# A two-block network on one core: memory for each high part of the Hyena spectrum, and the rotated query tile first

## The chip, the cores and the metric
The kernel runs on one core of a Trainium2 chip, in one launch. The metric is device time in microseconds (us); lower is better. The engines are TensorE (PE, matmuls), VectorE (DVE), ScalarE (ACT), GpSimd (POOL) and SyncE (SP, which issues the DMAs). Each runs its own instruction stream in order, and they meet at semaphores.

## What is computed
One sequence of 512 tokens with 1024 features, in fp32, goes through two blocks. The first has a convolution beside a forgetting attention, a cross attention to a memory and an MLP. The second has two layers, and the change is in one part of each: latent attention (layer 1) and the Hyena mixer (layer 2). Cut to these:

```python
# latent attention: 8 heads, 128 plain and 64 rotated dimensions
q = (rms_norm_2(c_q, g_q) @ w_uq).reshape(b, s, MLA_HEADS, QK_NOPE_DIM + QK_ROPE_DIM)
q_nope = q[..., :QK_NOPE_DIM]
q_rope = apply_rope(q[..., QK_NOPE_DIM:], cos[:, :, None], sin[:, :, None])
...
sc = (jnp.einsum('bqhd,bkhd->bhqk', qn, k_nope) + jnp.einsum('bqhr,bkr->bhqk', qr, k_rope))
p = jax.nn.softmax(sc.astype(jnp.float32) * scale, axis=-1).astype(v.dtype)

# Hyena: a long convolution by spectra, of two orders, each followed by a gate
u = dwconv_centred(x @ w_in, w_short)
v, g1, g2 = jnp.split(u, 3, axis=-1)
z = v.astype(jnp.float32)
for o, gate in enumerate((g1, g2)):
    k_f = jnp.fft.rfft(two_sided_kernel(filt[:, o, 0], filt[:, o, 1]), n=n, axis=0)
    z_f = jnp.fft.rfft(z, n=n, axis=1)
    y = jnp.fft.irfft(z_f * k_f, n=n, axis=1)[:, :length]
    z = gate.astype(jnp.float32) * (y + d_bias[o].astype(jnp.float32) * z)
return z.astype(x.dtype) @ w_o
```

## The kernel before
**Three matmuls for one.** Every fp32 operand is split into a high part (rounded to `fp32r`, a copy by ACT) and a low part (the rest, a subtraction by DVE or POOL). `mm3` (L140) multiplies low by high, high by low and high by high into one PSUM bank. Weights come in chunks of up to 1 MB through two buffers `W32` (`CHUNKS` lists them in order, L44 to L62); for chunk n `weights(n)` is in four programs: SP loads it once the parts of chunk n-2 are made, ACT makes the high part, POOL the low part (DVE a half of it where n is in `SHARED`).

**Order of the work.** Five functions, `tensor_program`, `scalar_program`, `vector_program`, `pool_program` and `sync_program`, write the order of each engine by hand. A step that is moved in one of them moves past all that stands between. PSUM banks are taken in turn (`open_bank`), and a bank is opened when its last tenant has been read.

**Latent attention** runs over four pairs of heads. For pair p PE makes the query tiles m = 0, 1 (plain parts of the two heads) and m = 2 (the rotated part of both), copies of which are `QNH` and `QRS`. It then swaps halves of `QRS` by a matmul with `SWAP`, makes the keys (chunk `ukv`), and goes on with the transposes, the logits and the values of earlier and later heads. ACT's `nope(p)` first calls `weights` for the next chunk and then copies the two plain tiles, `query(p)` copies the rotated one. DVE's `turn_q(p)` rotates it, `rotated(p)` makes its low part.

**Hyena.** For each order o in (0, 1): PE transforms (`to_spectrum`), eight groups of row m and half c, each with a real and an imaginary bank. DVE multiplies a group with the filter's spectrum in four instructions (`products`, the filter rows lie in `KB`), POOL adds these in pairs into `YF[k]`, k = 2m and 2m+1, one instruction each. ACT copies the high part `YH[k]` (`y_high`), DVE subtracts the low part `YL[k]` (`y_low`); in order 0 it also makes the low part of the imaginary pieces of the inverse matrix (`inverse_low`). PE transforms back over eight output tiles m and eight steps k (`istep`), three matmuls of 256 columns each. From each tile DVE makes the new z, DVE or POOL (by `gated_here`) multiplies it by the gate, and in order 0 POOL folds it (`z_turn`) and PE transposes it for the next transform; in order 1 ACT and DVE split it into `HYH` and `HYL` for the output product with chunks `hy_o`. The four-slot rings of `YH` and `YL` lie in the memory of the transform's operand `ZH`, `ZL`, and the waits say so:

```python
if k >= 4:
    act.wait_ge(*at("y_used", o, k - 4))
elif k == 0:
    act.wait_ge(*at(*(("zi", 0, 7) if o else ("hy", 23))))
else:
    act.wait_ge(*at("zf", o, 3, 1, 1))
```

The residual input `X` is kept in DRAM during the block (its memory holds filter rows) and comes back with one DMA, `xl`. The SP queue issues in this order: filter rows of both orders (`load_kb`), `xl`, the four chunks `hy_o`, then the up-projection's chunks.

## Time and profile before

| | |
|---|---|
| median of 3 runs (lowest, highest) | 2204.59 us (2202.55, 2209.34) |
| the profiled execution's own time | 2210.78 us |
| its span | 2208.9 us |
| PE, DVE, POOL, ACT busy | 95%, 59%, 42%, 38% |
| chain that ended last | PE 64%, DVE 23%, ACT 9% |
| latent attention with its queries, keys and values | about 870 to 1056 us |
| Hyena, transforms to output product | about 1622 to 1797 us |

A busy share is time in which an engine ran an instruction; PE's matmuls are pipelined, so two that overlap are both shown in full length and the step from start to start is what one costs. In a timeline the bracket gives the idle time before an instruction and the engine whose signal ended it.

### The profile page before, as it was taken

Reading aid. Unit: us, or ns where it says so; the run is one execution under the profiler, and the core shown is the slowest. Engines: PE = TensorE matmul, PEld = TensorE weight load, DVE = VectorE, ACT = ScalarE, POOL = GpSimd, SP = SyncE. Lnnn points to the kernel's source line nnn. Section 1 sums busy time; section 2 is a strip of 40 time slices with the busy share of each in tenths; the row PEclk is TensorE's granted clock in tenths of the full one; section 3 lists DMA queues with packets and bytes.
Section 4 is the critical chain, followed back from the end, with each engine's and each line's share of the span. In section 5 each row is a group of like instructions: output and inputs, shape, how many; then the busy total and the mean of one; then the engine's idle time right before and its main releaser. Section 6 shows DMA issues by size and latency. Waiting matters only on the chain.

```text
span 2208.9 us, 23694 instructions
## 1 busy us (share of the span) xinstructions
PE 2105.8 (95%) x9729; PEld 1723.4 (78%) x9729; DVE 1313.9 (59%) x1649; ACT 833.4 (38%) x1207; POOL 934.8 (42%) x404
## 2 busy tenths in 40 slices
PE   8999999989999998999999999999998899999997
PEld 5677768778888887787878877878887687887786
DVE  7765871743234434654477786445668647777643
ACT  4633465651122224675333333233322234333322
POOL 4252145554444436112434444444666443443443
PEclk9999779989999998999899999989999999999998
DMA  5322112212222221112122222214231212222221
GB/s 192 146 102 76 39 39 96 77 58 96 96 95 96 96 96 48 50 31 74 58 76 96 96 96 96 96 58 181 96 124 58 96 58 77 95 96 96 96 96 39
DMA packets 34272, 191.96 MB, mean 87 GB/s; under 512 B 3871, under 2 KB 4463, under 8 KB 14900
## 3 DMA queue, kind: packets, MB, share of 16 engines
q1 hardware_dynamic: 34164, 190.44, 24.7%
q8 instruction: 77, 1.26, 0.2%
q14 instruction: 31, 0.25, 0.0%
HBM read 176.72 MB, written 13.64 MB: 86 GB/s over the span
## 4 chain that ended last, share of the span: by engine, by line
PE 64%; DVE 23%; ACT 9%; issue 2%; POOL 1%; DMA 1%; SPq 0%; ACTq 0%; DVEq 0%; POOLq 0%
PE ps L136 58%; DVE TMP L165 9%; DVE TMP L171 6%; PE ps L135 4%; ACT WH L152 4%; ACT TMP L153 1%; ACT PAD L152 1%; PE ps L144 1%; DVE TMP L159 1%; DVE X L171 1%; DVE VG L159 1%; DVE X L159 1%; DVE ps L171 1%; DVE YL L159 1%; POOL WL L159 1%
## 5 line engine op out<-in xcount | busy, mean ns | idle before, releaser
L159 POOL TENSOR_TENSOR WL<-W,WH 128x2048 fp32r<-128x2048 f32 (+3 forms) x157 | 661.3, 4214 | 983.6 <-ACT WH L152 983.6
L136 PE MATMUL ps<-HH,WL 128*128 128x512 f32 (+1 forms) x1408 | 556.0, 395 | 27.1 <-DVE HL L159 7.7
L136 PE MATMUL ps<-HL,WH 128*128 128x512 f32 (+1 forms) x1408 | 547.1, 389 | 0.0
L136 PE MATMUL ps<-HH,WH 128*128 128x512 f32 (+1 forms) x1408 | 546.6, 388 | 0.0
L152 ACT ACTIVATE WH<-W 128x2048 fp32r<-128x2048 f32 (+2 forms) x148 | 274.7, 1856 | 334.0 <-PE ps L136 326.5
L136 PEld LDWEIGHTS ps<-HH,WL 128*128 128x128 f32 x1408 | 271.0, 193 | 95.2 <-issue 30.9
L136 PEld LDWEIGHTS ps<-HH,WH 128*128 128x128 f32 x1408 | 270.7, 192 | 53.7
L136 PEld LDWEIGHTS ps<-HL,WH 128*128 128x128 f32 x1408 | 271.2, 193 | 50.5 <-issue 0.2
L159 DVE TENSOR_TENSOR MRL<-MID,MRH 128x512 fp32r<-128x512 f32 x76 | 177.4, 2365 | 162.4 <-ACT MRH L152 162.4
L165 DVE TENSOR_SCALAR TMP<-PAD,PAR 128x512 f32<-128x512 f32 x88 | 208.9, 2374 | 76.2 <-ACT PAD L152 76.2
L136 PE MATMUL ps<-MRH,WL 128*128 128x512 f32 x608 | 238.5, 392 | 4.5 <-DVE TMP L171 2.3
L136 PE MATMUL ps<-MRH,WH 128*128 128x512 f32 x608 | 236.8, 389 | 0.0
L136 PE MATMUL ps<-MRL,WH 128*128 128x512 f32 x608 | 236.7, 389 | 0.0
L136 PEld LDWEIGHTS ps<-MRH,WL 128*128 128x128 f32 x608 | 114.2, 188 | 29.9 <-ACT PAD L152 3.1
L171 DVE SCALAR_TENSOR_TENSOR TMP<-PAD,PAR,TMP 128x512 f32<-128x512 f32 x176 | 132.3, 752 | 6.2
L136 PEld LDWEIGHTS ps<-MRH,WH 128*128 128x128 f32 x608 | 114.2, 188 | 24.0
L136 PEld LDWEIGHTS ps<-MRL,WH 128*128 128x128 f32 x608 | 114.2, 188 | 23.8 <-issue 0.5
L152 ACT ACTIVATE PAD<-ps 128x512 f32<-128x512 f32 x88 | 51.5, 588 | 182.8 <-PE ps L136 182.8
L159 POOL TENSOR_TENSOR TMP<-TMP,TMP 128x512 f32<-128x512 f32 x47 | 62.1, 1322 | 86.7 <-ACT TMP L153 85.0
L153 ACT ACTIVATE TMP<-TMP 128x512 f32<-128x512 f32 (+1 forms) x54 | 32.8, 608 | 163.5 <-DVE TMP L171 147.3
L171 DVE SCALAR_TENSOR_TENSOR X<-X,ps 128x512 f32<-128x512 f32 (+1 forms) x36 | 22.6, 628 | 118.3 <-PE ps L136 118.2
L159 DVE TENSOR_TENSOR TMP<-ps,TMP 128x512 f32<-128x512 f32 x36 | 24.8, 690 | 112.3 <-PE ps L136 105.6
(355 smaller groups left out, 3348.8 us busy)
## 6 DMA issues: line engine op xcount, KB each, us to landing
W<-in_up SPq DMA_DIRECT2D x44, 1024.0 KB, 4.8
W<-in_down SPq DMA_DIRECT2D x22, 1024.0 KB, 4.8
W<-in_w_up SPq DMA_DIRECT2D x16, 1024.0 KB, 4.8
W<-in_w_down SPq DMA_DIRECT2D x16, 1024.0 KB, 4.8
W<-in_hy_in SPq DMA_DIRECT2D x12, 1024.0 KB, 4.8
kd<-STG SPq DMA_DIRECT2D x36, 256.0 KB, 2.0
KB<-kd SPq DMA_DIRECT2D x8, 1024.0 KB, 5.1
W<-in_win_ag SPq DMA_DIRECT2D x4, 1024.0 KB, 4.8
```

The source lines that it names most:

```text
L135: return self.eng.matmul(out, lhs, rhs, start=start, stop=stop, skip_group_check=True)
L136: return self.eng.matmul(out, lhs, rhs, start=start, stop=stop)
L144: return QUIET if self.eng is None else self.eng.transpose(out, src, ident)
L152: return self.eng.activation(out, src, fn, scale=scale)
L153: return self.eng.activation(out, src, fn, scale=scale, bias=bias)
L159: return QUIET if self.eng is None else self.eng.tensor_tensor(out, a, b, op)
L165: return self.eng.tensor_scalar(out, a, s1, None, o1)
L171: return self.eng.scalar_tensor_tensor(out=out, in0=a, scalar=s, in1=b, op0=o1, op1=o2)
```

## The change
- Hyena: `ZH`, `ZL` have one place for both orders, and so has `YF`. `YL` has the memory of `YF` and is written over it. `YH` has eight buffers for each order, in memory of used weight buffers and filter rows; what each waits for follows. ACT makes six high parts before the output chunk's, not four.
- DVE makes `YL` 1 to 3 after product group 6 (index 5), and the products of groups 7 and 8 come after them. PE takes output tiles (0 to 3), (4, 5), (6, 7) over the first four steps instead of (0 to 3), (4 to 7).
- Filter rows of order 1 go to other buffers, with other waits. POOL starts with output chunk 0 after `yh(1,7)`. DVE gates tiles 0, 3, 7 of order 1 instead of 3 and 7.
- SP loads `hy_o` 0 once the first filter row of order 1 is used, `hy_o` 1 after the first four steps, and `X` in two halves after the inverse transform, ahead of `hy_o` 2 and 3.
- Latent attention: PE makes tile 2 first, then 0 and 1; ACT copies the rotated tile ahead of `nope`.

```diff
...
         for name in ("par", "idt", "mk", "zf", "f1", "fw", "dec", "wf", "e0", "e000", "e001", "e010", "e011",
-                     "tri", "mem", "pos", "swap", "xs", "xl",
+                     "tri", "mem", "pos", "swap", "xs", "xl0", "xl1",
                      *[f"x{k}" for k in range(8)], *[f"aug{q}{g}" for q in range(4) for g in range(2)],
...
         KX = [sb(f"KX{o}", (36, A + 112)[o], [128, 1024]) for o in range(2)]
-        AT = [A + 80, A]
-        ZH = [sb(f"ZH{o}", AT[o], [128, 4, 1024], R) for o in range(2)]
-        ZL = [sb(f"ZL{o}", AT[o] + 16, [128, 4, 1024], R) for o in range(2)]
-        YF = [sb(f"YF{o}", AT[1 - o], [128, 8, 1024]) for o in range(2)]
+        ZH = sb("ZH", A + 80, [128, 4, 1024], R)
+        ZL = sb("ZL", A + 96, [128, 4, 1024], R)
+        YF = sb("YF", A, [128, 8, 1024])
+        YL = sb("YL", A, [128, 8, 1024], R)
         KB = [sb(f"KB{i}", 8 * i, [128, 2048]) for i in range(4)]
-        YH = [[sb(f"YH{o}{i}", AT[o] + 8 * i if i else 32, [128, 1024], R) for i in range(4)] for o in range(2)]
-        YL = [[sb(f"YL{o}{i}", AT[o] + 8 * i + 4 if i else 36, [128, 1024], R) for i in range(4)] for o in range(2)]
+        _w = [16 + 8 * (CH[name][0] % 2) for name in ("dft_z", "dft_i")]
+        YH = [[sb(f"YH{o}{k}", at_, [128, 1024], R) for k, at_ in enumerate((32, 36, _w[o], _w[o] + 4, 0, 4, 8, 12))]
+              for o in range(2)]
         HYH = sb("HYH", A + 80, [128, 8, 512], R)
...
-            return m if o else m % 2
+
+            return 2 + (CH["dft_z"][0] + m) % 2 if o and m < 2 else m % 2
...
-            return m % 4 == 3 if o else m % 2 == 0
+            return m in (0, 3, 7) if o else m % 2 == 0
...
                 wh, wl = chunk(n)
-                for m in range(3):
+                for m in (2, 0, 1):
                     ps = open_bank("uq", p, m)
...
                                      k == 0, k == 2)
-                    ins.then_inc(*up(acc, ("uq", p, m), *[("w_used", n)] * (m == 2)))
-                    if p == 0 and m == 1:
+                    ins.then_inc(*up(acc, ("uq", p, m), *[("w_used", n)] * (m == 1)))
+                    if p == 0 and m == 0:
                         spread("nv", slot=20)
...
                     ins = pe.mm3(ps[:], wh[:, col:col + 128], wl[:, col:col + 128],
-                                 ZH[o][:, odd + kt, half(c)], ZL[o][:, odd + kt, half(c)], kt == 0, kt == 1)
+                                 ZH[:, odd + kt, half(c)], ZL[:, odd + kt, half(c)], kt == 0, kt == 1)
                 ins.then_inc(*up(acc, ("zf", o, m, part, c), *[("w_used", n)] * (o and m == 3 and part * c)))
...
                     pe.wait_ge(*at("yh", o, k))
-                    return pe.mm3(pss[m][:, 256 * h:256 * h + 256], YH[o][k % 4][:, blk(m)], YL[o][k % 4][:, blk(m)],
+                    return pe.mm3(pss[m][:, 256 * h:256 * h + 256], YH[o][k][:, blk(m)], YL[:, k, blk(m)],
                                   wh[:, col:col + 256], wl[:, col:col + 256], k == 0, k == 7, shared=True)
...
-                for q in range(0, 8, 4):
-                    for m in range(q, q + 4):
+                for tiles in ((0, 1, 2, 3), (4, 5), (6, 7)):
+                    for m in tiles:
                         pss[m] = open_bank("zi", o, m)
                     for k in range(4):
-                        for m in range(q, q + 4):
+                        for m in tiles:
                             ins = istep(m, k)
-                        if q:
-                            ins.then_inc(*up(acc, ("y_used", o, k)))
+                ins.then_inc(*up(acc, ("y_used", o, 3)))
                 for k in range(4, 7):
...
                 if p < 3:
+                    query(p + 1)
                     nope(p + 1)
-                    query(p + 1)
                     mla_k(p + 1)
...
                 if o == 1:
-                    act.wait_ge(*at("yh", 0, 7))
+                    act.wait_ge(*at("zf", 0, 3, 1, 1))
                 p3 = bank("tz", o, j)[:].rearrange("p (a c) -> p a c", a=4)
-                high(ZH[o][:, :, blk(j)], p3, ("zh", o, j))
+                high(ZH[:, :, blk(j)], p3, ("zh", o, j))
...
                 act.wait_ge(*at("yf", o, k, 1))
-                if k >= 4:
-                    act.wait_ge(*at("y_used", o, k - 4))
-                elif k == 0:
-                    act.wait_ge(*at(*(("zi", 0, 7) if o else ("hy", 23))))
-                else:
-                    act.wait_ge(*at("zf", o, 3, 1, 1))
-                high(YH[o][k % 4][:], YF[o][:, k, :], ("yh", o, k))
+                if o == 1:
+                    act.wait_ge(*at("zi", 0, 7))
+                if k in (2, 3):
+                    act.wait_ge(*(at("kbu", 1, 1) if o else at("w_low", CH["dft_z"][0])))
+                if k > 3:
+                    act.wait_ge(*at("kbu", o, k // 2))
+                high(YH[o][k][:], YF[:, k, :], ("yh", o, k))
...
                 act.wait_ge(*at("z2", 1, k))
-                act.wait_ge(*at("yh", 1, 7))
+                act.wait_ge(*at("zf", 1, 3, 1, 1))
                 act.copy(HYH[:, k, 0:256], VG[0][:, k, 0:256]).then_inc(*out(("hz", k, "hi1")))
...
             for o in range(2):
-                for k in range(4):
+                for k in range(6):
                     y_high(o, k)
...
                     weights(CH["hy_o"][0])
-                for k in range(4, 8):
-                    y_high(o, k)
+                y_high(o, 6)
+                y_high(o, 7)
                 for m in range(8):
...
                 p3 = bank("tz", o, j)[:].rearrange("p (a c) -> p a c", a=4)
-                low(ZL[o][:, :, blk(j)], p3, ZH[o][:, :, blk(j)], ("zh", o, j), ("free", "tz", o, j))
+                low(ZL[:, :, blk(j)], p3, ZH[:, :, blk(j)], ("zh", o, j), ("free", "tz", o, j))
...
             def y_low(o, k):
-                low(YL[o][k % 4][:], YF[o][:, k, :], YH[o][k % 4][:], ("yh", o, k))
+
+                low(YL[:, k, :], YF[:, k, :], YH[o][k][:], ("yh", o, k))
...
                         z_low(1, 7)
-                    if i == 3:
-                        y_low(o, 0)
-                    if i == 5 and o == 0:
-                        inverse_low(1)
-                    if i == 6:
-                        y_low(o, 1)
-                for k in range(2, 8):
+                    for k in {3: (0,), 5: (1, 2, 3)}.get(i, ()):
+                        y_low(o, k)
+                        if k % 2 and o == 0:
+                            inverse_low(k)
+                for k in range(4, 8):
                     if k % 2 and o == 0:
...
             hy_low(7)
-            dve.wait_ge(*at("xl"))
+            dve.wait_ge(*at("xl0"))
             for n in range(6):
...
                     weights(CH["hy_o"][1])
+                if n == 4:
+                    dve.wait_ge(*at("xl1"))
                 deep(2, "ho", n)
...
                         pool.wait_ge(*at("hy", 23))
-                    pool.tt(YF[o][:, 2 * m, half(c)], q[0], q[1], ALU.subtract).then_inc(
+                    pool.tt(YF[:, 2 * m, half(c)], q[0], q[1], ALU.subtract).then_inc(
                         *out(("yf", o, 2 * m, c), ("tf", "q", o, m, c, 0), ("tf", "q", o, m, c, 1)))
                     pool.wait_ge(*at("yi", o, m, c))
-                    pool.tt(YF[o][:, 2 * m + 1, half(c)], q[2], q[3], ALU.add).then_inc(
+                    pool.tt(YF[:, 2 * m + 1, half(c)], q[2], q[3], ALU.add).then_inc(
                         *out(("yf", o, 2 * m + 1, c), ("tf", "q", o, m, c, 2), ("tf", "q", o, m, c, 3)))
                 if o:
+                    pool.wait_ge(*at("yh", 1, 7))
                     weights(CH["hy_o"][0])
...
                 if o and m >= 2:
-                    n = CH["dft_z"][0] if (CH["dft_z"][0] - m) % 2 == 0 else CH["dft_i"][0]
+                    sp.wait_ge(*at("zi", 0, 7))
+                elif o and m:
+                    n = CH["dft_i"][0]
                     sp.wait_ge(*at("w_high", n))
                     sp.wait_ge(*at("w_low", n))
-                    if n in SHARED:
-                        sp.wait_ge(*at("w_low2", n))
+                    sp.wait_ge(*at("w_low2", n))
                 elif o:
-                    sp.wait_ge(*at("kbu", 0, m + 2))
+                    sp.wait_ge(*at("y_used", 0, 3))
                 elif m >= 2:
...
             sp.wait_ge(*at("kbu", 1, 0))
-            sp.wait_ge(*at("kbu", 1, 1))
-            load("xl", X[:], XD)
-            for m in (2, 3):
-                sp.wait_ge(*at("kbu", 1, m))
-            weights(*range(CH["hy_o"][0], len(CHUNKS)))
+            weights(CH["hy_o"][0])
+            sp.wait_ge(*at("y_used", 1, 3))
+            weights(CH["hy_o"][1])
+            sp.wait_ge(*at("zi", 1, 7))
+            load("xl0", X[:, 0:4, :], XD[:, 0:4, :])
+            load("xl1", X[:, 4:8, :], XD[:, 4:8, :])
+            weights(*range(CH["hy_o"][2], len(CHUNKS)))
             for k in range(8):
```

## Rows read from the trace of the kernel before

**Rows 1.** The page, PE's granted clock in 40 slices of the span, tenths of full speed
```profile
PEclk9999779989999998999899999989999999999998
```

**Rows 2.** Hyena windows: busy us of PE, PEld, DVE, ACT, POOL; PEclk, DMA
```profile
1645.00:1665.00 20.00, 16.71 (x114) 16.07 (x113) 14.20 (x17) 6.11 (x6) 6.76 (x4) 0.83 0.44 167
...
1705.00:1728.00 23.00, 16.34 (x121) 14.89 (x120) 17.51 (x14) 9.00 (x8) 14.42 (x9) 1.00 0.28 96
```

**Rows 3.** Waits from 1600 to 1800 us: who waited for whom, total us, times, longest
```profile
PE ps L135 <- DVE YL L159: 9.9, 9, 2.0
```

**Rows 4.** PE timeline, latent attention: start, us, instruction, idle before and its releaser
```profile
929.12 1.10 PE L136 MATMUL ps<-QRS,SWAP 128*128 128x512 f32 x2 [0.78 <-ACT QRS L152]
...
999.65 0.50 PE L136 MATMUL ps<-KRL,QR 128*128 128x512 f32 x1 [0.65 <-DVE QR L159]
```

**Rows 5.** ACT timeline, Hyena block
```profile
1643.91 2.95 ACT L152 ACTIVATE YH<-YF 128x1024 fp32r<-128x1024 f32 x3 [11.56 <-PE ps L136]
...
1754.62 1.91 ACT L152 ACTIVATE WH<-W 128x2048 fp32r<-128x2048 f32 x1 [2.65 <-PE ps L136]
```

**Rows 6.** PE timeline, inverse transform of order 0
```profile
1647.26 0.40 PE L135 MATMUL ps<-WH,YL 128*128 128x256 f32 x1 [2.02 <-DVE YL L159]
...
1647.46 0.41 PE L135 MATMUL ps<-WL,YH 128*128 128x256 f32 x1
...
1663.01 0.28 PE L135 MATMUL ps<-WL,YH 128*128 128x256 f32 x1
...
1663.13 0.28 PE L135 MATMUL ps<-WH,YH 128*128 128x256 f32 x1
...
1663.87 0.36 PE L135 MATMUL ps<-WH,YL 128*128 128x256 f32 x1 [0.46 <-DVE YL L159]
```

**Rows 7.** DVE timeline, Hyena block
```profile
1640.52 2.49 DVE L159 TENSOR_TENSOR TMP<-ps,KB 128x512 f32<-128x512 f32 x4 [0.20 <-POOL YF L159]
...
1658.14 1.23 DVE L159 TENSOR_TENSOR YL<-YF,YH 128x1024 fp32r<-128x1024 f32 x1 [4.84 <-ACT YH L152]
...
1659.29 0.42 DVE L159 TENSOR_TENSOR WL<-W,WH 128x256 fp32r<-128x256 f32 x1
...
1701.47 2.49 DVE L159 TENSOR_TENSOR TMP<-ps,KB 128x512 f32<-128x512 f32 x4 [0.20 <-POOL YF L159]
...
1719.72 8.18 DVE L159 TENSOR_TENSOR YL<-YF,YH 128x1024 fp32r<-128x1024 f32 x4 [4.61 <-ACT YH L152]
...
1728.63 0.75 DVE L171 SCALAR_TENSOR_TENSOR VG<-VG,SM,ps 128x512 f32<-128x512 f32 x1 [0.72 <-PE ps L135]
...
1749.32 2.10 DVE L159 TENSOR_TENSOR HYL<-VG,HYH 128x256 fp32r<-128x256 f32 x6
```

**Rows 8.** POOL timeline, Hyena block
```profile
1632.70 2.56 POOL L159 TENSOR_TENSOR YF<-TMP,TMP 128x512 f32<-128x512 f32 x2 [0.25 <-DVE TMP L159]
...
1641.89 10.00 POOL L159 TENSOR_TENSOR YF<-TMP,TMP 128x512 f32<-128x512 f32 x6 [0.20 <-DVE TMP L159]
...
1718.82 8.00 POOL L159 TENSOR_TENSOR WL<-W,WH 128x512 fp32r<-128x512 f32 x4 [4.79 <-ACT WH L152]
```

**Rows 9.** The chain that ended last, in order of time: start, us, what
```profile
1681.67 4.34 PE ps L136 x12
...
1689.76 16.60 PE ps L136 x72
```

**Rows 10.** DMA issues: line, engine, count, KB each, us to landing
```profile
X<-xd SPq DMA_DIRECT2D x1, 2048.0 KB, 7.8
```

**Rows 11.** DVE timeline, latent attention, head pair 0
```profile
894.94 1.41 DVE L171 SCALAR_TENSOR_TENSOR TMP<-CQF,PAR,ps 128x512 f32<-128x512 f32 x2 [1.27 <-PE ps L135]
...
899.37 0.69 DVE L159 TENSOR_TENSOR TMP<-ps,CS 128x512 f32<-128x512 f32 x1
```

**Rows 12.** POOL timeline, latent attention
```profile
958.11 2.39 POOL L159 TENSOR_TENSOR WL<-W,WH 128x1024 fp32r<-128x1024 f32 x1 [25.33 <-ACT WH L152]
...
994.45 4.60 POOL L159 TENSOR_TENSOR WL<-W,WH 128x2048 fp32r<-128x2048 f32 x1 [2.15 <-ACT WH L152]
```

## The prediction

> **What bounds the kernel now.** I read the page first: TensorE (PE) is busy for 95% of the span, and its clock is granted nearly in full except in some slices [rows 1]. So time is to be had only where PE stands still or runs at the lower clock. I took windows through the two stretches that the diff touches. In the Hyena block PE is busy for 16.7 of 20 us, and 16.3 of 23 us, while VectorE (DVE) or GpSimd (POOL) is not [rows 2]. The list of waits of 1600 to 1800 us names DVE's low parts of the spectrum, `YL`, as the cause [rows 3]. The PE timeline then gives places. In latent attention the gaps are small and end on the copy of the rotated query, or on `QR` [rows 4].
>
> **Hyena, order 0.** Before, PE finishes the forward transform at about 1643.7 and starts the inverse transform, but high parts 1 to 3 lie in memory that the transform reads, so ScalarE (ACT) copies them only then [rows 5], and DVE takes `YL1` after product group 7, `YL2` and `YL3` after group 8. High parts 4 to 7 wait until PE has used buffers 0 to 3. PE stands 2.02 us for `YL1`, again for `YL2`, then runs for 31 matmuls at a step of 0.20 to 0.21 us instead of 0.12, the lower of the clock's two levels (1.2 GHz for 2.4), and starts the last step of tile 0 at 1663.87 [rows 6].
> Changed: all eight high parts have memory of their own, so ACT follows POOL's sums at once, and DVE does `YL1` to `YL3` after group 6. Prices: a group of four products 2.49 us, `YL` 1.15 us to the start of the next instruction (1659.29 less 1658.14), the low part of a piece of the inverse matrix 0.42 busy, 0.33 to the next start [rows 7], one POOL sum 1.28 (half of 2.56), one matmul of 256 columns 0.12, so 117 of them (8 tiles x 4 steps x 3, three more steps for two tiles, the last for one: 96+18+3) are 14.0 us [rows 6, 8].
> What shares something: POOL's six sums of groups 6 to 8 took 10.00 us instead of 6 x 1.28 = 7.7 while DVE did its `YL` [rows 8]. Both have their two inputs in SBUF. I let such instructions exclude each other and alternate: a `YL` beside a waiting sum costs about 1.27 more.
> DVE ends group 6 at 1643.0 [rows 7]. `YL1` waits 0.15 for POOL and ends at 1644.4; a sum goes between, to 1645.6; inverse low 1, `YL2`, `YL3`, inverse low 3 end at 1648.6 (0.33+1.15+1.15+0.33). Groups 7 and 8 are put back from here and end at 1653.5 (2 x 2.45). `YL4` waits for one sum and ends at 1654.9, a sum to 1656.1, then two inverse lows and `YL5` to `YL7`: 2 x 0.33 + 3 x 1.15 = 4.1, to 1660.3. PE: steps 0 to 3 of tiles 0 to 3 are done at 1650.2, tiles 4 and 5 need the banks of group 7 (1651.1), tiles 6 and 7 follow, to 1657.0; the last step of tile 0 starts at 1660.4. That is 3.4 us before 1663.87; DVE ends last. Below it: 0, if PE runs at the low level again and DVE alternates with POOL at every `YL`; above: 5.9, if PE alone set it (1643.7 + 14.0 + 0.3 = 1658.0). The chain that follows (DVE, POOL's turns, PE's transposes) starts with tile 0 and moves whole. I take 3.4.
> The Trainium skill ("SBUF — State Buffer", on the shared port pair) says that a VectorE instruction with two SBUF inputs and a GpSimd one that reads SBUF take the pair exclusively, for the whole instruction; the trace agrees (10.00 against 7.7 us). If the two only shared a bandwidth pool, without turns, order 0 would come at about 5.9 instead of 3.4 us; it speaks against putting three `YL` in front of products.
>
> **Order 1.** The forward transform ends at 1706.4 (1689.76 + 16.60) [rows 9], in old times. After group 6 (1701.47 + 2.49, less the 0.1 that two instructions overlap: 1703.9 [rows 7]) DVE does `YL1` at 1705.3, a POOL sum, `YL2` 1707.8, `YL3` 1708.9, groups 7 and 8 to 1713.8, `YL4` 1715.2, a sum, `YL5` to `YL7` to 1719.9. There are no inverse lows here. PE needs 14.0 us from 1706.6: 1720.7, so it is just PE that ends last. Before, ACT waited for the output chunk's DMA (the load was behind group 8) and four `YL` took 8.18 us (4 x 1.15 without that) beside POOL's four low parts of that chunk, 8.00 us [rows 7, 8]; the chunk is now loaded after the first row of spectra and POOL waits for `yh(1,7)`. First tile seen by DVE: 1728.63 before [rows 7], 1720.9 now: 7.7 us.
> Paid back in the tail: DVE now gates tile 0, one more of its instructions (0.76), and POOL's low parts of the chunk (4.60 us for such a chunk alone [rows 12], now from 1719.9) lie beside that gate, both with two inputs in SBUF: about 0.5 more. DVE's own chain from 1728.63 to the last three `HYL` at 1749.32 [rows 7] remains the bound of the output product, PE waits for it. Net 7.7 - 1.3 = 6.4. Bounds: 4 (one more alternation in each of the two tiles, and the gate fully late) to 8.
>
> **Waits added, edits at nothing.** POOL's wait for `yh(1,7)` has its low part of output chunk 0 and five gates behind it; PE needs that low part when the inverse is done (1729.7 in old times), it is there at about 1725. SyncE's wait for `y_used(1,3)` and for `zi(1,7)` has `hy_o` 1, both halves of `X`, and `hy_o` 2 and 3 behind it: the 2 MB of `X` landed in 7.8 us [rows 10], with the 1 MB of chunk 2 at that rate 11.7 after the inverse transform, which ended near 1737.3 (tile 0 at 1728.3, then 75 matmuls of 0.12). ACT's copy of chunk 2 came 17.3 us after that, at 1754.62 [rows 5], and the first residual just before: hidden, with 5 us to spare. An overrun would be paid in full. Filter rows (1,0) and (1,1) are now loaded after `y_used(0,3)`, about 1657, 2 MB like `X`, so some 8 us; the products of order 1 start beside PE's run at 1681.67 [rows 9]. Rows (1,2) and (1,3) come after `zi(0,7)`, near 1677, and are used 15 us later. An in-place `YL` is not in the trace; the nearest row is `YL` into other memory, 1.23 us [rows 7]. I take the same and leave 0.1 us either way for each, 1.6 at most over sixteen, little of it on the path. Tile order (4,5), (6,7) has the same matmuls.
>
> **Latent attention.** Pair 0: the rotated tile ends two tiles earlier, so PE's swap no longer waits for its copy, and the key latents' high parts no longer stand behind `QRS` on ACT. DVE's rotation, which starts at 899.37 behind `CVL`, can start at about 897.65 (894.94 + 1.41 [rows 11], and two `CVL` at 0.65 behind ACT's copies, which overlap the 1.41): 1.7 us, and the first logits hang on DVE from there. Pairs 1 to 3: PE is idle for 0.78 us before the swap at 929.12 [rows 4], 0.94 counted from the point at which the next pipelined matmul could have started (928.18); this goes. Next late: the low part of the `ukv` chunk, since ACT's copy of it now stands behind `QRS` (0.5 us). It ended at 958.11+2.39 = 960.5, then 961.0, while PE would want it at 960.5 [rows 12]: pair 2 keeps 0.5. In pair 3 DVE's `QR` is held by POOL's 4.60 us low part of the output chunk from 994.45, which doesn't move, and PE already waits 0.65 for it [rows 4, 12]: the gain is lost there, 0. Sum 1.7+0.9+0.5+0 = 3.1; from 1 (pair 0 half) to 4.6 (1.8 + 3 x 0.94).
>
> **Sum.** 3.4 + 6.4 + 3.1 = 12.9 us. The profiled execution took 2210.78, so 2197.9 on its terms; it is 6.2 above the median of the runs shown, 2204.59, and on that the forecast is 2191.7. About 0.3%, 6.6 us, is what a measurement can tell from no change.
>
> **Rivals.**
> - *The low clock comes back.* A pause of 2.02 us went before the 0.20 us steps in order 0, yet in order 1 PE stood 6.7 of 23 us and was granted full clock (0.83 and 1.00 [rows 2]). PE's pauses get shorter, which speaks against it. Price: 31 matmuls x 0.09 = 2.9 us in order 1, half of that in order 0 where DVE ends last: 12.9 - 4.4 = 8.5, so 2196.1. The 12 matmuls that took 4.34 us instead of 2.7 [rows 9] could as well lose that: 1.6 less, 2190.
> - *DVE and POOL don't take turns as I let them*: order 0 gives 5.9, so 2189.2.
> - *The gain of one part is taken back.* `YL1` to `YL3` move the products, so PE waits for banks before tiles 4 and 6 instead of for `YL`. That holds if POOL's sums delay `YL1` by more than a sum each; then order 0 and most of order 1 give 4 in place of 9.8, with 3.1: 2197.5. That the change does nothing but the attention part: 2201.5. For it: DVE is full in both cases, 17.5 of 23 us.
> - *Slower.* PE's clock stays low over the whole block. It did so elsewhere with PE busy all the time: two slices of 55 us are granted 0.7 to 0.8 [rows 1]. From the inverse transform of order 0 to the last output tile are 154 us; at 0.78 against about 0.95 now that is 154 x 0.17 = 26 us lost, 2218. It beats the gain once more than 13 us, half of that, are lost (a granted clock of 0.87 or less over the block). Against: the 512-column streams around were at full clock.
>
> **Chances.** Forecast 0.62 (alone 2187 to 2196), low clock 0.14, no turns 0.10, taken back 0.10 (half of it within 0.3%), slower 0.04. Faster by over 0.3%: 0.62 + 0.14 + 0.10 + 0.05 less 0.03 for the tails, 0.88; within 0.3% 0.08; slower 0.04. The range: from 18.5 us (4.6+5.9+8), 2186, and a little of a better clock, 2185, to 5.0 (1+0+4), 2199.6.
>
> **What would show it.** Right: `YH` of order 0 starts from about 1632 on one by one and none waits for PE; no pause of PE over 1.2 us in an inverse transform; first tile of order 0 out some 3 us earlier relative to the forward transform's end (20.2 us before), of order 1 14 to 15 instead of 22 us; four `YL` of order 1 in about 6 instead of 8.2 us; no pause before the swap in pairs 1 to 3. Wrong: PE waiting over 2 us for `zf` banks at tiles 4 or 6, a granted clock under 0.9 in these 20 us, residuals waiting for `X`, or output chunk 2 landing after chunk 0 is used.

## The result, and the profile after

| | before | after |
|---|---|---|
| median, us (lowest, highest; 14 runs each) | 2206.63 (2201.17, 2214.91) | 2194.05 (2186.92, 2198.88) |
| the profiled execution's own time / its span | 2210.78 / 2208.9 | 2188.62 / 2186.4 |

The ratio after to before is 0.9937, 95% interval 0.9924 to 0.9950: 13.9 us less by the ratio, 12.6 between the two medians. Forecast were 12.9 us and 2191.7 us, with 2185 to 2199.6 as the range; faster by over 0.3% had 0.88. The direction was right, and the time and the size of the gain are near. Experiments 1 and 2 had one execution each at a far lower granted clock (2626.45 us at 0.738, 7690.57 us at 0.416), and their ratios leave these two out.

The two profiled executions differ by 22.5 us, which is more than the change is worth. The chains of both show where the rest comes from: a stage that the change doesn't touch, long before latent attention, starts its run of matmuls 8 us earlier (506.79 us before, 498.77 after). Up to it the same code was granted another clock; four equal blocks of matmuls took 66.5 us before (214.30 to 280.79) and 60.1 after (213.38 to 273.48), 6.4 of the 8 us. First the kernel before, then after, by windows (columns as in [rows 2]):

```profile
165.00:220.00 55.00, 55.00 (x226) 42.73 (x224) 33.60 (x57) 19.06 (x33) 16.99 (x4) 0.91 0.22 77
220.00:275.00 55.00, 55.00 (x217) 43.09 (x217) 44.30 (x82) 26.75 (x60) 9.15 (x2) 0.78 0.11 39
```
```profile
165.00:220.00 55.00, 55.00 (x241) 43.55 (x240) 35.76 (x62) 19.73 (x35) 17.59 (x4) 0.97 0.22 77
220.00:275.00 55.00, 55.00 (x245) 42.71 (x243) 49.16 (x86) 27.87 (x64) 9.12 (x2) 0.88 0.14 46
```

PE is busy for 55.00 of 55 us in all four lines, but gets through more matmuls at the higher clock (226 and 217 before, 241 and 245 after). So the two spans must not be subtracted. I compare stretches between the same two instructions instead, which start and end inside the changed stages:

| stretch, us | before | after | forecast |
|---|---|---|---|
| latent attention: first query matmul to the first of its output product | 136.32 | 132.98 | -3.1 |
| order 0: first inverse matmul to DVE's first `VG` | 20.85 | 17.05 | -3.4 |
| first `VG` of order 0 to the first inverse matmul of order 1 | 41.69 | 41.71 | 0 |
| order 1: first inverse matmul to DVE's first `VG` | 22.44 | 14.23 | -7.7 |
| from there to PE's first sum over the new residual `X` | 26.08 | 27.53 | +1.3 |

The sum is -3.3 - 3.8 - 8.2 + 1.4 = -13.9 us. That the ratio gives the same 13.9 is in part chance: its interval is 11.0 to 16.8 us.

Now the rows. The page's clock line answers to [rows 1]: the fifth slice, 7 before, is 8 now. It is the second of the two windows above; a slice is some 55 us.

```profile
PEclk9999879989999998999899999999999999999998
```

The same two Hyena stretches, in windows (after's order 0 starts 11.65 us earlier). PE is busy for 18.25 of 20 and for 23.00 of 23 us, where it was 16.71 and 16.34 [rows 2], and the granted clock is full:

```profile
1632.00:1652.00 20.00, 18.25 (x145) 17.43 (x143) 18.86 (x24) 3.89 (x4) 8.47 (x6) 1.00 0.28 102
1691.00:1714.00 23.00, 23.00 (x193) 22.98 (x192) 21.67 (x29) 7.17 (x10) 14.30 (x10) 1.00 0.14 46
```

ACT's timeline: high parts of order 0 follow POOL's sums (the bracket names `YF`); none waits for PE, as three did in [rows 5].

```profile
1625.20 1.06 ACT L152 ACTIVATE YH<-YF 128x1024 fp32r<-128x1024 f32 x1 [3.29 <-POOL YF L159]
...
1631.65 1.06 ACT L152 ACTIVATE YH<-YF 128x1024 fp32r<-128x1024 f32 x1 [3.19 <-POOL YF L159]
```

PE's timeline holds all its pauses in the inverse transform of order 0; the longest is 0.59 us (2.02 in [rows 6]):

```profile
1634.14 0.38 PE L135 MATMUL ps<-WH,YL 128*128 128x256 f32 x1 [0.54 <-DVE WL L159]
...
1639.23 0.36 PE L135 MATMUL ps<-WH,YL 128*128 128x256 f32 x1 [0.53 <-DVE TMP L159]
...
1648.42 0.36 PE L135 MATMUL ps<-WH,YL 128*128 128x256 f32 x1 [0.59 <-DVE YL L159]
```

DVE's timeline has the order that the prediction priced. The ends are 1632.65, 1636.69, 1641.83 and 1648.28; the forecast, less the 11.65, was 1632.75, 1636.95, 1641.85 and 1648.65:

```profile
1631.31 1.34 DVE L159 TENSOR_TENSOR YL<-YF,YH 128x1024 fp32r<-128x1024 f32 x1
1632.57 1.51 DVE L159 TENSOR_TENSOR WL<-W,WH 128x256 fp32r<-128x256 f32 x1
1634.01 2.35 DVE L159 TENSOR_TENSOR YL<-YF,YH 128x1024 fp32r<-128x1024 f32 x2
1636.28 0.41 DVE L159 TENSOR_TENSOR WL<-W,WH 128x256 fp32r<-128x256 f32 x1
...
1698.27 5.85 DVE L159 TENSOR_TENSOR YL<-YF,YH 128x1024 fp32r<-128x1024 f32 x4
```

The four `YL` of order 1 take 5.85 instead of 8.18 us [rows 7], and the transform of order 1 is now a chain of PE alone (the chain of waits, where 14.05 us are one piece):

```profile
1666.24 4.34 PE ps L136 x12
...
1674.35 16.57 PE ps L136 x72
1690.92 14.05 PE ps L135 x117
```

In latent attention PE's swap of pair 1 has no idle time in its bracket, where [rows 4] had 0.78; pairs 2 and 3 are like it. The wait for `QR` in pair 3 is 1.25 instead of 0.65 us:

```profile
918.39 1.02 PE L136 MATMUL ps<-QRS,SWAP 128*128 128x512 f32 x2
...
988.18 0.50 PE L136 MATMUL ps<-KRL,QR 128*128 128x512 f32 x1 [1.25 <-DVE QR L159]
```

### The profile page after: what moved, and what is told of

It is laid out like the page before. It is cut to its first block, busy times and chain, and to the rows that moved or that the text cites. A ratio compares the mean times of both kernels' runs of the same rounds, so it can differ in the third digit from the quotient of the medians.

```text
span 2186.4 us, 23689 instructions
## 1 busy us (share of the span) xinstructions
PE 2095.8 (96%) x9729; PEld 1716.0 (78%) x9729; DVE 1310.3 (60%) x1650; ACT 833.7 (38%) x1207; POOL 931.8 (43%) x403
## 4 chain that ended last, share of the span: by engine, by line
PE 63%; DVE 24%; ACT 10%; issue 1%; POOL 1%; DMA 0%; ACTq 0%; SPq 0%; DVEq 0%; POOLq 0%
PE ps L136 58%; DVE TMP L165 9%; DVE TMP L171 6%; PE ps L135 4%; ACT WH L152 4%; ACT TMP L153 1%; ACT PAD L152 1%; DVE ps L171 1%; PE ps L144 1%; DVE VG L159 1%; DVE TMP L159 1%; DVE X L171 1%; DVE X L159 1%; ACT PA L150 1%; ACT PA L153 1%
```

## Experiments

Stretches are those of the table above, read in each experiment's own trace. Experiments 3 to 9 have one profiled execution each, so their times say nothing and the stretches must do. Where one of experiments 2 to 11 leaves order 0, order 1 or the stretch between them alone, it agrees with its base kernel within 0.05 us; experiment 1 is off by up to 0.55. The attention stretch is less steady. In ten executions with the attention edits eight took 132.95 to 133.12 us, and two that do not touch it (experiments 3 and 6) took 134.1. Behind the same pauses of 0.28 to 0.79 us at the end of the last softmax the granted clock stayed at 1.00 in the kernel after and fell in those two. Three us of it, from 129.0 us behind the first query matmul on, in the kernel after and in experiment 6 (columns as in [rows 2]):

```profile
1010.45:1013.45 3.00, 2.83 (x17) 2.28 (x16) 2.83 (x5) 1.72 (x4) 0.00 (x0) 1.00 0.00 0
```
```profile
1019.85:1022.85 3.00, 3.00 (x14) 2.83 (x13) 2.51 (x5) 2.15 (x4) 0.00 (x0) 0.57 0.00 0
```

So one execution can be 1.1 us longer in a stretch by its clock alone.

**1. The attention edits alone**, on the kernel before.

```diff
-                for m in range(3):
+                for m in (2, 0, 1):
...
-                    nope(p + 1)
                     query(p + 1)
+                    nope(p + 1)
```

> The kernel before with the attention edits alone. Theory (the two parts are independent and each gives what its stretch shows): time 3.4 us under before, the attention stretch (PE's 102-matmul run to its 74-matmul run) 183.1 us instead of 186.6, the Hyena stretch unchanged at 161.1. Rival (the whole gain is in Hyena, and attention's is taken back by the FFN, whose chunks are paced by DMA and ACT): the stretch is shorter, the time within 1 us of before.

Measured: ratio 0.9972 (0.9955 to 0.9989), 6.2 us, with 3.8 to either side, so the time alone can't tell 3 from 10, but it leaves out the rival's 1 us. The attention stretch is 133.03 us, 3.3 less than before; the inverse transforms take 21.00 and 22.99, within 0.6 us of the kernel before.

**2. The Hyena edits alone**: the kernel after with the same lines put back.

```diff
-                for m in (2, 0, 1):
+                for m in range(3):
...
+                    nope(p + 1)
                     query(p + 1)
-                    nope(p + 1)
```

> The changed kernel with the attention edits undone. Theory: 10.5 us under before, the Hyena stretch (last 72-matmul run of the input product to the 72-matmul run of the output product) 150.6 instead of 161.1 us, attention 186.6. Rival as for the attention part alone: 14 us under before, because all of it is Hyena.

Measured: ratio 0.9937 (0.9919 to 0.9955). Attention 136.38 us, as before; order 0 17.02 and order 1 14.23, as after. The two parts are additive: -3.3 and -10.5 us, since neither stretch hides the other. The stretches show this; the ratio does not. It equals that of the whole change, 13.9 us, and its interval holds both the rival's 14 and the theory's 10.5. Against the rival speak the attention stretch, here and in experiment 1, and experiment 1's interval.

**3. The memory without DVE's new order** of `YL`.

```diff
-                    for k in {3: (0,), 5: (1, 2, 3)}.get(i, ()):
-                        y_low(o, k)
...
-                for k in range(4, 8):
+                    if i == 3:
+                        y_low(o, 0)
...
+                    if i == 6:
+                        y_low(o, 1)
+                for k in range(2, 8):
```

> The changed kernel with DVE's old order of the low parts (YL1 after group 7, YL2 and YL3 after group 8); memory, waits and PE's tiles as changed. Theory (DVE's order is needed, because PE stands for YL1 to YL3): PE waits about 2 us before step 1 and 1 to 2 us before step 2 in both orders, tile 0 of order 1 is out 3 us later than in the changed kernel; Hyena stretch 154 us. Rival (memory alone gives the gain, DVE does the same work in any order and ends last with YL7): 150.6 to 151.5 us.

Measured: order 0 20.14 and order 1 18.82 us; with the tail 6.9 us are lost, twice the 3.4 that I had expected. The rival (memory alone gives the gain) is out. Against the kernel before, all that is left of the Hyena edits here (early high parts, the tile split, chunk 0 loaded earlier, POOL's wait) gives 0.7 and 3.6 us, and DVE's order gives 3.1 and 4.6. Of the 4.6 some 1.7 (an estimate) came through the clock: behind a pause of 1.93 us the granted clock was 0.62 and 0.81 over 6 us, that is 3 x 0.38 + 3 x 0.19. The kernel before has the same pause in order 1 and kept 1.00 behind it, so in another execution DVE's order could show as 2.9. PE's timeline (this kernel's) still waits for `YL1`, as in [rows 6], though the high part had been there:

```profile
1638.72 0.40 PE L135 MATMUL ps<-WH,YL 128*128 128x256 f32 x1 [2.00 <-DVE YL L159]
```

**4. Tiles (0 to 3), (4 to 7)** as before.

```diff
-                for tiles in ((0, 1, 2, 3), (4, 5), (6, 7)):
+                for tiles in ((0, 1, 2, 3), (4, 5, 6, 7)):
```

> The changed kernel with output tiles (0 to 3), (4 to 7). Theory (tiles 6 and 7 need banks of product group 8): in order 0 PE waits for group 8 before any matmul of tiles 4 and 5, about 2.9 us instead of 0.5, but DVE's YL7 ends last anyway, so order 0 is 0 to 1 us later; in order 1 PE has no slack and loses 1 to 1.5 us. Hyena stretch 151.5 to 153. Rival (banks are free in time): 150.6.

Measured: order 0 19.99, order 1 16.25 us, 2.9 and 2.0 more than after. I had expected 0 to 1 and 1 to 1.5: in order 0 it is PE now that ends last, with no pause for `YL7`. And the prediction had called the order of tiles free. It is not: with four tiles at once PE needs all banks of groups 7 and 8 before it goes on, and these are read late now, because `YL1` to `YL3` stand in front of them. The timeline of PE in this kernel:

```profile
1646.62 0.35 PE L135 MATMUL ps<-WH,YL 128*128 128x256 f32 x1 [3.27 <-DVE TMP L159]
...
1706.10 0.36 PE L135 MATMUL ps<-WH,YL 128*128 128x256 f32 x1 [1.79 <-DVE TMP L159]
```

In order 0 the granted clock of the 3 us behind the pause was 0.54, of the next 0.89: some 1.7 us of the 2.9 (an estimate) are clock (3 x 0.46 + 3 x 0.11), the rest the pause.

**5. POOL does not wait for `yh(1,7)`** before output chunk 0.

```diff
                 if o:
-                    pool.wait_ge(*at("yh", 1, 7))
                     weights(CH["hy_o"][0])
```

> The changed kernel without POOL's wait for yh(1,7), so its four low parts of output chunk 0 run beside YL4 to YL7 of order 1. Theory (two instructions with both inputs in SBUF take turns, whole): the four YL take about 8.2 us as before instead of 5.9, tile 0 of order 1 is 2 us later; the tail is 1 us shorter since POOL is free for the gates: Hyena stretch 151.5. Rival (they share bandwidth or don't disturb each other; the 8.2 us of before came from the late DMA): YL stay at 5.9, stretch 149.5 to 150.6.

Measured: order 1 16.27 instead of 14.23 us, and the tail 0.7 shorter. DVE's four `YL` and POOL's four low parts again take 8 us each, as in the kernel before; 5.6 us of it they lie side by side. DVE (the four, then the last of them alone), then POOL:

```profile
1705.62 8.04 DVE L159 TENSOR_TENSOR YL<-YF,YH 128x1024 fp32r<-128x1024 f32 x4
...
1711.36 2.30 DVE L159 TENSOR_TENSOR YL<-YF,YH 128x1024 fp32r<-128x1024 f32 x1
```
```profile
1708.08 7.98 POOL L159 TENSOR_TENSOR WL<-W,WH 128x512 fp32r<-128x512 f32 x4
```

They take turns, one instruction each. The rival without turns is out. (The Trainium skill, "SBUF — State Buffer", section "Who interferes with whom", has it that the order of issue decides who of the two blocks, for the whole instruction; the trace agrees: the first `YL` takes 1.27 us to the next start, and the three that must let a POOL instruction of 1.3 us pass take 2.2 to 2.3 us instead of 1.15.)

**6 and 7. All gates of order 1 on DVE; and gates 3 and 7 alone**, as before the change.

```diff
-            return m in (0, 3, 7) if o else m % 2 == 0
+            return True if o else m % 2 == 0
```

> The changed kernel with all eight gates of order 1 on DVE. Theory (turns at the port: a HYL pair beside a POOL gate costs 1.8 to 2.6 us instead of 0.76): DVE takes 5 gates more, 5 x 0.65 = 3.2 us, and saves 1.8 + 3 x 1.06 = 5.0: the tail is 1.8 us shorter, stretch 148.8. Rival (work moved to the engine that is the bound costs its duration): 3.2 us longer, 153.8.

> The changed kernel with DVE's gates as before, tiles 3 and 7 only. Theory (my price of 0.76 for DVE's gate of tile 0 is real but POOL isn't free yet: its low parts of chunk 0 end 2.5 us after that gate is wanted): tile 0's high part comes about 4 us later, HYL of tile 0 delays everything behind it on DVE: stretch 151.5 to 153. Rival (the gate on DVE is a plain loss): 149.9.

Measured from the first `VG` of order 1 to PE's first sum over `X`: after 27.53 us, all gates 26.90, two gates 28.33. So the rival of experiment 6 (3.2 us longer) is out, and so is that of experiment 7 (the gate on DVE is a plain loss). All three have DVE as their end; a gate that moves costs DVE 0.69 us and saves it the turn that a `HYL` pair takes beside a gate on POOL. The third pair of `HYL` in the kernel after, then with all gates on DVE (DVE's timelines):

```profile
1716.89 1.82 DVE L159 TENSOR_TENSOR HYL<-VG,HYH 128x256 fp32r<-128x256 f32 x2
```
```profile
1729.07 0.75 DVE L159 TENSOR_TENSOR HYL<-VG,HYH 128x256 fp32r<-128x256 f32 x2
```

Each of the middle tiles takes DVE 2.84 instead of 3.18 us. The gain, 0.6 us, is a third of the 1.8 that I had expected: DVE has five more gates, and one of them takes 1.49 us beside POOL's low parts. With two gates DVE stands for tile 0's high part, whose gate on POOL comes behind the low parts. That is the cause which the theory named; the whole costs 0.8 us where it had 0.9 to 2.4:

```profile
1718.89 2.48 DVE L159 TENSOR_TENSOR HYL<-VG,HYH 128x256 fp32r<-128x256 f32 x2 [1.59 <-ACT HYH L152]
```

**8. POOL's low part of attention's output chunk 0 in four pieces**, so that DVE's `QR` waits for a piece, not for the whole.

```diff
-PIECES = {CH["w_mq"][1], CH["w_mo"][0], CH["hy_o"][0], *THIRD}
+PIECES = {CH["mla_o"][0], CH["w_mq"][1], CH["w_mo"][0], CH["hy_o"][0], *THIRD}
```

> The changed kernel with POOL's low part of mla_o chunk 0 in four pieces of 512 columns. Theory (in pair 3 QR waits for the whole 4.6 us instruction): QR's two instructions take at most 2 us instead of 2.96 and start at once, PE's wait of 1.25 us before the first logits with QR falls to 0 to 0.3, the attention stretch 182.0 instead of 183.1. Rival (the wait has another cause, such as ACT's QR): unchanged.

Measured: PE's wait for `QR` fell from 1.25 to 0.48 us, and the attention stretch stayed, 133.12 against 132.98, where the theory had 1.1 us less. DVE's pair of `QR` is no shorter (2.96 after, 3.17 here): the first of the two takes 1.47 us instead of 2.24, but the second, beside the next piece, 1.67 instead of 0.69; the next instruction of the chain, `PAL`, starts 3.20 us behind the start of the first `QR` instead of 3.00. Half of the theory fell: POOL's big instruction makes PE wait for `QR`, but what sets the end is DVE behind it. DVE's timeline, first after, then here:

```profile
985.88 2.96 DVE L159 TENSOR_TENSOR QR<-TMP,QR 64x512 fp32r<-64x512 f32 x2
988.88 2.48 DVE L159 TENSOR_TENSOR PAL<-ps,PAH 128x512 fp32r<-128x512 f32 x4
```
```profile
993.31 3.17 DVE L159 TENSOR_TENSOR QR<-TMP,QR 64x512 fp32r<-64x512 f32 x2
996.51 2.48 DVE L159 TENSOR_TENSOR PAL<-ps,PAH 128x512 fp32r<-128x512 f32 x4
```

**9. The kernel before with PE's pause for `YL1` filled** in order 0: 12 matmuls of the first inverse step are done twice, which leaves the values as they are. It asks whether the low clock of [rows 6] cost anything.

```diff
                         for m in range(q, q + 4):
                             ins = istep(m, k)
+                        if (o, q, k) == (0, 0, 0):
+                            for m in range(4):
+                                istep(m, 0)
```

> The kernel before; in order 0 PE repeats the first inverse step of tiles 0 to 3 (12 matmuls of 256 columns that start their accumulation anew, so the values stay) in the place where it paused 2.02 us for YL1. Theory: the low level of PE's clock came with that pause and set part of the time, since high parts 4 to 7 wait for PE. Then the pause is some 0.6 us, the granted clock of 1647 to 1653 (0.57 and 0.50) is near 1.00, the steps are 0.12 instead of 0.20 us, and the first tile of order 0 comes 2 to 2.8 us earlier (20.85 us from the first inverse matmul in the kernel before). Rival 1: the clock falls for another reason than the pause: 0, or up to 1.4 us later. Rival 2: the clock comes back but DVE ends last anyway: within 0.5 us.

Measured: the pause is 0.60 us, the granted clock 1.00 from there to the end of order 0, and the first `VG` comes after 20.51 instead of 20.85 us: 0.3, rival 2. The time went into other waits. PE's timeline here; in the kernel before the second pause was 0.81 and there was no third:

```profile
1641.55 0.36 PE L135 MATMUL ps<-WH,YL 128*128 128x256 f32 x1 [0.60 <-DVE YL L159]
...
1645.09 0.39 PE L135 MATMUL ps<-WH,YL 128*128 128x256 f32 x1 [1.88 <-DVE YL L159]
...
1647.74 0.36 PE L135 MATMUL ps<-WH,YL 128*128 128x256 f32 x1 [0.96 <-DVE YL L159]
```

**10. The kernel after with PE's pause ahead of order 1 filled.** Before and after alike, PE pauses 2.3 us for the last folded tiles, and the 12 matmuls behind it take 4.34 us [rows 9].

```diff
                 ps = open_bank("tz", o, j)
+                if (o, j) == (1, 5):
+                    for i in range(16):
+                        pe.turn(ps[:, blk(i % 4)], IDT[:], IDT[:])
                 pe.wait_ge(*at("zs", o, j))
```

> The kernel after; PE transposes the identity 16 times into the bank that it has already opened for folded z tile 5 of order 1, in the place where it pauses 2.32 us at the end of order 0 and after which 12 matmuls of 512 columns took 4.34 us. These 16 take about 1.6 us at 0.1 each, so the pause is about 0.7. Theory: the low clock came with the pause, and PE sets the time here: 12 matmuls in about 2.8 instead of 4.34 us, and from the first VG of order 0 to the first inverse matmul of order 1 1.5 us less (41.7 us in the kernel after). Rival 1: the clock is low whatever PE does in the pause: no change. Rival 2: the clock is full but DVE's products pace the forward transform: under 0.5 us. Rival 3: the bank isn't free, the 16 come after the pause and delay: 1 us and more lost.

Measured: from the first `VG` of order 0 to the first inverse matmul of order 1 40.07 instead of 41.71 us, 1.6 less, and nothing is lost later. Experiment 11, a second execution with the same filler, has 40.07 again. The theory holds. PE's timeline, first after, then here:

```profile
1665.61 0.63 PE L144 MATMUL ps<-IDT,TMP 128*128 128x128 f32 x4 [2.32 <-DVE ZL L159]
1666.00 0.48 PE L136 MATMUL ps<-ZH,WL 128*128 128x512 f32 x1
...
1667.49 0.63 PE L136 MATMUL ps<-ZL,WH 128*128 128x512 f32 x1
1667.92 0.63 PE L136 MATMUL ps<-ZH,WH 128*128 128x512 f32 x1
```
```profile
1662.21 1.91 PE L144 MATMUL ps<-IDT 128*128 128x128 f32 x16
1664.59 0.66 PE L144 MATMUL ps<-IDT,TMP 128*128 128x128 f32 x4 [0.47 <-POOL TMP L159]
1665.01 0.47 PE L136 MATMUL ps<-ZH,WL 128*128 128x512 f32 x1
...
1666.24 0.39 PE L136 MATMUL ps<-ZH,WH 128*128 128x512 f32 x1
1666.47 0.40 PE L136 MATMUL ps<-ZH,WL 128*128 128x512 f32 x1
```

A step is 0.43 us behind the idle pause and 0.23 behind the filled one. (The Trainium skill, "TensorE: Matmul & The Clock Gate", section "HAM oscillation — how this bites in real kernels", has a kernel whose idle gaps between bursts of matmuls make each next burst start at the low clock. The trace agrees in that, though the gaps of its example are longer than the 2.32 us here; the measurement decides.) The median was 2191.1 us, ratio 0.9930 (0.9907 to 0.9954).

**11. Experiments 6 and 10 together**, the best version by stretches.

> The kernel after with both: the 16 transposes of the identity in PE's pause and all eight gates of order 1 on DVE. If both hold, 1.5 + 0.6 = 2.1 us less than the kernel after on like terms, some 0.1%; ratio to the kernel before near 0.9925 to 0.993. If the filled pause gives nothing, 0.6 us less, not to be told from the kernel after by the medians.

Measured: 2.2 us less than after from the start of the Hyena transforms to PE's first sum over `X` (120.03 against 122.28), as expected. Its median, 2195.4 us, with a ratio of 0.9937 (0.9915 to 0.9959), can't show that (I had expected 0.9925 to 0.993), and neither can that of experiment 10: the intervals of both hold the kernel after. Both are well under the kernel before; that they beat the kernel after is shown for the stretch and not for the whole time.

## Why the prediction was right, and where it was not

**What bounds.** Right. PE's idle time in the two transforms was what could be had, and `YL` was behind it: in the list of waits from 1580 to 1780 us of the kernel after the three waits that replace the 9.9 us of [rows 3] sum to under 2 us. The low clock, named beside the idle time, was worth little in order 0 (experiment 9).

**Order 0, 3.4 forecast, 3.8 measured.** The chain of DVE that I wrote down came within 0.4 us at its end, and the last step of tile 0 waits 0.59 us for it. Experiment 9 shows that the low clock had cost only 0.3 us here, which was no term of the sum either.

**Order 1, 7.7 forecast, 8.2 measured.** The forecast had PE and DVE end nearly together; measured, DVE ends at 1704.12, PE at 1704.97. Experiments 3, 4 and 5 take one edit each out of the whole: without DVE's order 4.6 us are lost, without the split 2.0, without POOL's wait 2.0 (0.7 of which the tail gives back). They overlap, so they can't be added. One edit of the sum was not tried alone, the earlier load of output chunk 0. That it is part of the gain is argued from the chain of the kernel before, in which this piece stands between the products and ACT's high part of chunk 0, with `YL4` to `YL7` behind:

```profile
1712.03 4.78 DMA W<-in_hy_o
```

In the kernel after the chunk is issued at 1679.39, 11.4 us before the inverse transform of order 1 starts, and no longer in the chain. What it is worth by itself stays open.

**The tail, 1.3 forecast, 1.4 measured.** The size is right, one of its two places is not. The moved gate costs 0.74 us and is not held by POOL's low parts of the chunk, for which the forecast had put 0.5. These push POOL's own gates back, and the first `HYL` pair beside them takes 2.58 us instead of 1.85. That the 0.7 came out near the 0.5 is luck.

**Attention, 3.1 forecast, 3.3 measured; its terms less well.** Measured from the first query matmul, pair 1's swap comes 2.66 us earlier (1.7 + 0.9, as forecast), pair 2's 3.68, so pair 2 keeps 1.0 and not 0.5, and pair 3's 4.31. Then `QR` gives 0.9 back: [rows 12]'s low part of the output chunk holds it, as forecast, and it takes more than pair 3 had won (0.6). That low part starts 3.4 us earlier, counted from the first query matmul, and 3.3 is what the stretch keeps. An error of 0.5 and one of 0.3 nearly cancelled, which is luck.

**What was priced wrongly: the tile order.** "Tile order (4,5), (6,7) has the same matmuls" put it at nothing. Experiment 4 gives 2.9 and 2.0 us for it, 4.7 with the tail. The sum came out right because I had worked PE's path with the new order (tiles 4 and 5 at the banks of group 7) and so had it in the two terms; but as an edit it was not free, and "the gain of one part is taken back" is just what happens without it: PE waits 3.27 and 1.79 us for banks.

**Edits at nothing.** `X` in two halves and `hy_o` 2 arrive in time: ACT's copy of chunk 2 has the same idle time ahead of it as in [rows 5] (2.64 against 2.65 us). No wait of SP that the change adds shows in a stretch; POOL's for `yh(1,7)` is 0.7 us of the tail (experiment 5).

**The rivals.** The low clock didn't come back in the inverse transforms, and no turns is refuted by experiment 5. The slower case, the block at a low clock, had no sign of itself: the windows have 1.00. Three slips in the prediction changed nothing: 31 x 0.09 is 2.8 and not 2.9; 17.5 of 23 us is not a full DVE (it is 21.67 of 23 now); and in the second of the two slices at 0.7 to 0.8 PE was busy for 50.6 of 55 us, not all the time. The forecast time was 2.4 us under the median: the kernel before came out at 2206.63 over more runs, 2.0 above the figure that I started from, and the medians differ by 12.6 and not 12.9.

## What to carry to other kernels

A low part or a copy that many later steps need goes ahead of work that only frees buffers, provided that the consumer is split so that it needs few of those buffers at a time; price the two together, since of the 10.5 us in Hyena 5.9 were left without the split, and 3.7 without the early low parts. Before a VectorE instruction with two SBUF inputs is put on the critical path, look at what GpSimd does beside it, and delay that if it has slack. Compare stretches between like instructions; two profiled executions can differ by more than the change.

## What the runs showed of the hardware that I had not expected

- PE's clock and the pause before. Behind pauses of 2.00, 2.02, 2.3 and 3.27 us PE ran at the low level (1.2 GHz) for some 3 to 7 us; behind the 2.3 ahead of order 1 it did so in each of the kernels that have it. Behind 1.88, 1.79 and 1.54 us, in the same stages, it kept 2.4 GHz, and behind 1.93 us it did both: kept it in the kernel before (order 1), lost it in experiment 3. And a run of pauses of 0.28 to 0.79 us in attention lost it in experiments 3 and 6 and kept it in the kernel after. So the length of the one pause does not decide alone, and not even the same code with the same pauses does; what else does was not tried. Useless work in the pause kept the clock: transposes gave 1.6 us where PE set the time (experiment 10), repeated matmuls 0.3 us where DVE did (experiment 9).
- With PE busy for all of 55 us the granted clock of the same code was 0.91 and 0.78 in one execution, 0.97 and 0.88 in another. That is worth some 6.4 of the 8 us between the two, and no experiment here moved or explained it.
- A VectorE instruction that reads PSUM is not held by GpSimd: in the kernel after the groups of four products (one input from PSUM) take 2.47 to 2.56 us beside POOL's sums. A `YL`, with both inputs in SBUF, takes 1.34 instead of 1.21 even where it only meets the end of a sum.
